# Prompt attention's transposed keys: one straight copy each, the swapped halves by on-chip transfers, and other places for a table load and four masks

## The chip, the cores and the metric

The kernel runs on one core of one Trainium2 chip. The metric is the device time of one execution in microseconds (us). A core has TensorE (PE, with its weight loads listed as PEld), VectorE (DVE), ScalarE (ACT), GpSimd (POOL) and SyncE (SP), which run their own instruction queues in order and meet through semaphores, and 16 DMA engines that all queues share.

## The reference, cut to what matters

One inference step of a two-layer decoder, for a prompt of 512 tokens and 8 sample tokens. Layer 0 is native sparse attention with 16 query heads of 64 dimensions in 4 groups that share a key and value head. The change concerns the prompt's attention alone. Each query sees three branches, which are gated and added:

```python
s_c = jnp.einsum('bqkgd,bckd->bkgqc', qg, kc) * scale       # compressed keys, 31 of them
p_c = masked_softmax(s_c, mask_c)
...
s_s = jnp.einsum('bqkgd,bkqnpd->bkgqnp', qrg, k_sel) * scale   # selected blocks
p_s = masked_softmax(s_s.reshape(...), mask_s)
...
s_w = jnp.einsum('bqkgd,blkd->bkgql', qrg, kw) * scale      # window of 512
p_w = masked_softmax(s_w, mask_w)
```

With 512 prompt tokens there are 8 blocks and 16 may be selected, so the selected branch and the window branch are both plain causal attention, over different keys (`kind` 0 and 1 below).

## The kernel before, in words

Layer 0's attention is a row of blocks: projections, compression of the cached keys, prompt attention, sample attention. At the end of each block all engines meet. The change is inside `stage_prompt_attention` (L2268).

**Units.** The softmax work is cut into 64 units, `NU`. A unit n is a pair of query heads (`hp`, 8 of them), a `kind` (0 or 1) and a query tile `i` of 128 rows, in the order 3, 0, 2, 1 (`unit`, L2321). So units 0 to 3 are kind 0 of the first pair, units 4 to 7 kind 1 of the first pair, and units 32 and up use key heads 2 and 3. The width of a unit is (i + 1) x 128 keys, hence 512, 128, 384 and 256. Both heads of a pair (`par` 0 and 1) are computed at once, one on the upper and one on the lower 64 rows of PE; so the transposed keys of a head, `kT`, 64 rows high, must exist in both halves of the 128 partitions.

**The path of a unit.** PE computes the scores (L2333) into one of three banks of PSUM; they wait for the DVE minimum of the unit before (L2330). DVE adds the causal mask and takes the minimum (L2487, the wait is on `scored`). ACT takes the exponential with its sum (L2546). DVE inverts the sum (L2494). POOL scales by the inverse and the gate (L2572). Four units later (`LAG`) PE turns the probabilities (L2347), DVE and ACT copy them back (L2430, L2522), and six or seven units later come the products with the values (L2364).

**Compressed branch.** Its scores for key head h are `scores_c(h)` (PE, L2394), its masks `mask_c(h)` (DVE, two additions per head, L2465), then `least_c`, `lower_c`, an exponential on ACT (L2551), `total_c`, `weight_c`, `weigh_c`. It is spread between the units.

**The opening.** PE turns the keys in four groups (L2387), one for each kind and pair of key heads, into four PSUM banks; rows 0 to 63 of a bank are the pair's first head, rows 64 to 127 its second. In the kernel before, DVE copies rows 0 to 63 of each bank to both halves of the first head's slot (L2457, eight copies of 64 rows), and ACT copies rows 64 to 127 to both halves of the second head's slot (L2529, eight copies), each bank after DVE has done with it. ACT then spreads the compressed values (L2532, four copies to `vcz`) and comes to its first exponential. PE's order is: compressed heads 0 and 1, unit 0, compressed head 2, unit 1, compressed head 3, units 2 and up. DVE does the masks of heads 0 and 1 after unit 1, that of head 2 after unit 2, that of head 3 after unit 3.

**SP's queue.** In this block SP first runs `cache.read_table(sp, "sp")` (L2577), which reads 4 x 8 = 32 page numbers from on-chip memory into registers (the value load is on L2697). Then it issues `first_selected` (16 transfers of 128 KB for the sample attention, L2712) and `first_windows` (L2715), and later ones behind semaphores of prompt attention's progress.

Of the kernel before, what the change touches and what calls it, by code (L numbers as in the profile page):

```python
# [19 lines left out]
P = 128  # L20
# [2247 lines left out]
def stage_prompt_attention(c, cache):  # L2268
# [10 lines left out]
    PR = 5  # L2279
    ORDER = (3, 0, 2, 1)  # L2280
    k_turned, k_kept, spread = c.sem("att_k_turned"), [c.sem("att_k_kept_dve"), c.sem("att_k_kept_act")], c.sem("attc_spread")
    cleared, v_spread = c.sem("attc_cleared"), c.sem("attc_v_spread")
    c_scored, c_masked, c_least, c_subbed, c_exped, c_link, c_weight, c_scaled, c_turned, c_kept = (
        c.sem(f"attc_{x}") for x in ("scored", "masked", "least", "subbed", "exped", "link", "weight", "scaled", "turned", "kept"))
# [4 lines left out]
    with ExitStack() as mine:  # L2289
# [16 lines left out]
        def wide(x):  # L2306
            return x.unsqueeze(2).to_broadcast([P, QT * GRP, KP])

        def score_bank(n, par):
            return (2 * n + par) % 3  # L2310

# [12 lines left out]
        with nc.Block() as block:  # L2324
            @block.tensor
            def _(pe):
                def scores(n):
                    hp, kind, i = unit(n)
                    if n >= 1:
                        pe.wait_ge(lowered, 2 * n - 1)  # L2330
                    for par in range(2):
                        rows = slice(par * HD, par * HD + HD)
                        mm = nc.tensor.matmul(ps[:, score_bank(n, par), 0:(i + 1) * P], c.qrT[rows, hp, i * P:(i + 1) * P],  # L2333
                                              kT[rows, kind, hp // 2, 0:(i + 1) * P], start=True, stop=True)
                    mm.then_inc(scored, 1)

                def turn(n):
# [51 lines left out]
                def scores_c(h):  # L2389
# [5 lines left out]
                                                  kcz[:, h].rearrange("p w k -> p (w k)"), start=True, stop=True)  # L2395
                    mm.then_inc(c_scored, 1)

                pe.wait_ge(spread, 2)
                scores_c(0)
                scores_c(1)  # L2400
                for e in range(2):
                    pe.wait_ge(k_kept[e], 4)
                scores(0)
                scores_c(2)
                for e in range(2):
                    pe.wait_ge(k_kept[e], 8)
                scores(1)
                scores_c(3)
                for n in range(2, NU + LAG_PV + 1):
                    if n < NU:  # L2410
                        scores(n)
                    if n == LAG:
                        pe.wait_ge(c_masked, 2 * NKV)
                    if LAG <= n < NU + LAG:
                        turn(n - LAG)
                    if n % (4 * QT) == 2 * QT and n < NU:
                        turn_c(n // (4 * QT))
                    for part in range(2):
                        m = n - LAG_PV - part
                        if m >= 0 and m % QT == QT - 1:  # L2420
                            values(m, part)

            @block.vector
            def _(dve):
# [25 lines left out]
                    dve.wait_ge(c_weight, h + 1)  # L2450
                    nc.vector.tensor_mul(rows_k(h), rows_k(h), wide(ctot[:, h])).then_inc(c_scaled, 1)

                for n in range(4):
                    kind, a = divmod(n, 2)
                    dve.wait_ge(k_turned, n + 1)
                    for to in range(2):
                        nc.vector.tensor_copy(kT[to * HD:(to + 1) * HD, kind, 2 * a, :], ps[0:HD, n, :]).then_inc(k_kept[0], 1)  # L2457
                def mask_c(h):

                    dve.wait_ge(c_scored, NKV)  # L2460
                    for j in range(2):
                        src = ps[:, 4 + h, j * QT * 2 * KP:(j + 1) * QT * 2 * KP].rearrange("p (t w k) -> p t w k", t=QT, w=2)
                        dst = sc[:, h].rearrange("p (t g k) -> p t g k", t=QT, k=KP)[:, :, 2 * j:2 * j + 2]
                        mask = c.cmask[:].rearrange("p (t k) -> p t k", t=QT).unsqueeze(2).to_broadcast([P, QT, 2, KP])
                        nc.vector.tensor_add(dst, src, mask).then_inc(c_masked, 1)  # L2465
# [13 lines left out]
                for n in range(NU + LAG):  # L2479
                    if n < NU:  # L2480
                        hp, kind, i = unit(n)
                        w = (i + 1) * P
                        dve.wait_ge(scored, n + 1)
                        for par in range(2):
                            if n >= PR:
                                dve.wait_ge(turned[par], n - PR + 1)
                            nc.vector.tensor_tensor_reduce(pr[:, n % PR, par, 0:w], ps[:, score_bank(n, par), 0:w], c.causal[:, SEQ - w:SEQ], 1.0,  # L2487
                                                           3e38, ALU.add, ALU.min, low[:, n % PR, par:par + 1]).then_inc(lowered, 1)
                    if n >= LAG:
                        keep_first(n - LAG)  # L2490
                    if 1 <= n <= NU:
                        m = n - 1
                        dve.wait_ge(exped, 2 * m + 2)
                        nc.vector.reciprocal(tot[:, m % PR], tot[:, m % PR]).then_inc(recip, 1)  # L2494
                    if n == 1:
                        mask_c(0)
                        mask_c(1)
                    if n == 2:
                        mask_c(2)
                    if n == 3:  # L2500
                        mask_c(3)
                    if n < NU:
                        h, r = divmod(n, 4 * QT)
                        if r == 1:
                            least_c(h)
                        if r == 2:
                            lower_c(h)
                        if r == QT:
                            total_c(h)
                        if r == QT + 1:  # L2510
                            weight_c(h)
                        if r == QT + 2:
                            weigh_c(h)

            @block.scalar
            def _(act):
                def keep_second(n):
                    act.wait_ge(turned[1], n + 1)
                    dst, src = turned_back(n, 1)
                    if n // QT >= 2:  # L2520
                        act.wait_ge(o_filled, n // QT - 1)
                    nc.scalar.copy(dst, src).then_inc(kept[1], 1)  # L2522

                for n in range(4):
                    kind, a = divmod(n, 2)

                    act.wait_ge(k_kept[0], 2 * (n + 1))
                    for to in range(2):
                        nc.scalar.copy(kT[to * HD:(to + 1) * HD, kind, 2 * a + 1, :], ps[HD:P, n, :]).then_inc(k_kept[1], 1)  # L2529
                act.wait_ge(cleared, 2)  # L2530
                for g in range(GRP):
                    nc.scalar.copy(vcz[32 * g:32 * g + NCP, :, g // 2, g % 2 * HD:(g % 2 + 1) * HD],  # L2532
                                   c.vcp[0:NCP, :].rearrange("p (h d) -> p h d", h=NKV)).then_inc(v_spread, 1)
                for n in range(NU + LAG_PV + 1):
                    if LAG <= n < NU + LAG:
                        keep_second(n - LAG)
                    if n % (4 * QT) == 2 * QT and n < NU:
                        h = n // (4 * QT)
                        act.wait_ge(c_turned, h + 1)
                        nc.scalar.copy(pcT[:, h, :], ps[:, 7, :]).then_inc(c_kept, 1)  # L2540
                    if n < NU:
                        hp, kind, i = unit(n)
                        w = (i + 1) * P
                        for par in range(2):
                            act.wait_ge(lowered, 2 * n + par + 1)
                            nc.scalar.activation(pr[:, n % PR, par, 0:w], pr[:, n % PR, par, 0:w], ACT.Exp, scale=-1.0,  # L2546
                                                 bias=low[:, n % PR, par:par + 1], accum_out=tot[:, n % PR, par:par + 1]).then_inc(exped, 1)
                    if n % (4 * QT) == QT - 1 and n < NU:
                        h = n // (4 * QT)
                        act.wait_ge(c_subbed, h + 1)  # L2550
                        nc.scalar.activation(sc[:, h], sc[:, h], ACT.Exp, scale=-1.0).then_inc(c_exped, 1)  # L2551
                    if n >= LAG_PV and (n - LAG_PV) % (2 * QT) == 0 and n > LAG_PV:
                        hp = (n - LAG_PV) // (2 * QT) - 1
                        act.wait_ge(o_filled, 2 * (hp + 1))
                        nc.scalar.copy(c.oT[:, hp, 0:SEQ], ps[:, 7, :]).then_inc(o_kept, 1)
# [20 lines left out]
            def _(sp):  # L2576
                cache.read_table(sp, "sp")  # L2577
                sp.wait_ge(c.h_stored, 16)
                cache.first_selected(sp)
                sp.wait_ge(k_turned, 4)  # L2580
                cache.first_windows(sp)
# [1421 lines left out]
```

## Time and profile before

| | us |
|---|---|
| median of 3 runs | 1520.79 |
| lowest and highest | 1518.48, 1522.76 |
| the profiled execution, its own time | 1520.4 |
| its span, first to last instruction | 1518.7 |
| PE busy, DVE busy, ACT busy | 1468.6, 872.3, 422.7 |

The profile is of one execution. The span is what the trace's clock covers; the execution's own time has some 1.7 us around it. Prompt attention lies between about 265 and 414 us of the span. Busy shares are means over stages with different limits; what counts for the change is which wait ends last in the stretch that it touches.

### The profile page before, as it was taken

What the parts mean: (1) busy time and instruction counts of PE and PEld (TensorE: products, weight loads), DVE (VectorE), ACT (ScalarE), POOL (GpSimd) and SP (SyncE); (2) the same over time, 40 slices, a digit from 0 to 9 for tenths busy, and PEclk for the clock granted to TensorE, in tenths of its full rate; (3) what the DMA queues carried; (4) which work ended last, traced back from release to release, by engine and by line L of the source; (5) the groups of instructions that cost most, each with busy time, mean ns of one, the idle gap of its engine ahead of it and who ended that gap; (6) DMA issues with size and microseconds to landing.
All of it is one profiled execution on the core that took longest, in us unless ns stands there. A gap on an engine that the chain in (4) does not pass through costs nothing. (4 is left out here: it accounts for less than half of the span.)

```text
span 1518.7 us, 25820 instructions
## 1 busy us (share of the span) xinstructions
PE 1468.6 (97%) x9697; PEld 1220.3 (80%) x9697; DVE 872.3 (57%) x1926; ACT 422.7 (28%) x1076; POOL 353.9 (23%) x478
## 2 busy tenths in 40 slices
PE   8999999899898999999999999899999999999998
PEld 7878899555565888888888888688888888888888
DVE  2754343778653796565567734671485556676513
ACT  3011343788630343333300000433441111000012
POOL 0000300466561339993000018280000000000000
PEclk9999999899999999999999999999999999999999
DMA  8445471311196626464343320703121312322201
GB/s 272 117 123 144 140 234 47 106 32 53 51 334 213 203 83 225 143 217 152 109 127 125 111 90 0 305 30 119 61 106 57 112 65 102 111 84 83 84 28 57
DMA packets 142893, 184.34 MB, mean 121 GB/s; under 512 B 31298, under 2 KB 101642, under 8 KB 141746
## 3 DMA queue, kind: packets, MB, share of 16 engines
q1 hardware_dynamic: 139634, 174.31, 35.2%
q0 software_dynamic: 3136, 8.39, 1.6%
q8 instruction: 77, 1.26, 0.3%
q14 instruction: 46, 0.38, 0.1%
HBM read 163.42 MB, written 29.69 MB: 127 GB/s over the span
## 5 line engine op out<-in xcount | busy, mean ns | idle before, releaser
L2572 POOL TENSOR_SCALAR att_p<-att_p,att_tot,gates 128x512 f32<-128x512 f32 (+3 forms) x128 | 79.4, 631 | 62.1 <-DVE att_tot L2494 62.1
L296 PE MATMUL psum<-xT,l_w 128*128 128x260 f32 x384 | 85.3, 383 | 2.0 <-PEq L113 1.8
L953 PE MATMUL psum<-xT,l_w 128*128 128x260 f32 x384 | 85.2, 383 | 1.6 <-PEq L113 1.6
L296 PEld LDWEIGHTS psum<-xT,l_w 128*128 128x128 f32 x384 | 72.8, 190 | 13.5 <-issue 2.4
L953 PEld LDWEIGHTS psum<-xT,l_w 128*128 128x128 f32 x384 | 72.8, 190 | 12.9 <-issue 1.8
L969 PE MATMUL psum<-l_up_t,l_w_sums 128*128 128x260 f32 x336 | 78.2, 382 | 0.0
L2487 DVE CUSTOM_DVE_ANT_0 att_p<-psum,causal 128x512 f32<-128x512 f32 (+3 forms) x128 | 57.4, 486 | 27.9 <-PE psum L2333 27.8
L2145 PE MATMUL psum<-cmp_xt,cmp_w 64*128 64x256 f32 (+1 forms) x640 | 72.2, 362 | 0.3 <-DVE cmp_xt L2066 0.3
L2546 ACT ACTIVATE att_p<-att_p,att_low 128x512 f32<-128x512 f32 (+3 forms) x128 | 70.8, 556 | 4.7 <-DVE att_low L2487 4.1
L969 PEld LDWEIGHTS psum<-l_up_t,l_w_sums 128*128 128x128 f32 x336 | 63.8, 190 | 9.8
L2333 PE MATMUL psum<-att_kT,qrT 64*128 64x512 f32 (+3 forms) x256 | 54.3, 503 | 14.1 <-DVE att_low L2487 13.9
L1232 ACT ACTIVATE l_hidden<-l_tmp 128x260 f32<-128x260 f32 x64 | 26.6, 420 | 144.9 <-DVE l_tmp L1382 144.8
L312 PE MATMUL psum<-xT,l_w 128*128 128x260 f32 x272 | 62.9, 382 | 0.0
L969 PE MATMUL psum<-xT,l_w 128*128 128x260 f32 x272 | 62.9, 382 | 0.0
L312 PE MATMUL psum<-l_up_t,l_up_w_sums 128*128 128x260 f32 x264 | 61.5, 382 | 0.0
L2145 PEld LDWEIGHTS psum<-cmp_xt,cmp_w 64*128 64x128 f32 x640 | 60.8, 187 | 0.6 <-DVE cmp_xt L2066 0.5
L969 PE MATMUL psum<-xT,l_w_sums 128*128 128x260 f32 x256 | 60.4, 382 | 0.0
L969 PEld LDWEIGHTS psum<-xT,l_w 128*128 128x128 f32 x272 | 51.7, 190 | 7.9
L1086 PE MATMUL psum<-l_hidden,l_w 128*128 128x260 f32 (+2 forms) x384 | 58.1, 311 | 0.0
L1715 PE MATMUL psum<-xT,proj_w 128*128 128x260 f32 x256 | 56.9, 383 | 0.7 <-DVE xT L1854 0.5
L312 PEld LDWEIGHTS psum<-xT,l_w 128*128 128x128 f32 x272 | 51.1, 190 | 7.5
L1086 PEld LDWEIGHTS psum<-l_hidden,l_w 128*128 128x128 f32 x384 | 53.8, 191 | 3.9
(584 smaller groups left out, 3179.9 us busy)
## 6 DMA issues: line engine op xcount, KB each, us to landing
l_w<-in_mlp_w SPq DMA_DIRECT2D x16, 2048.0 KB, 8.1
l_w<-in_mlp_w SPq DMA_DIRECT2D x32, 1024.0 KB, 5.1
proj_w<-in_nsa_w_in SPq DMA_DIRECT2D x4, 2048.0 KB, 10.4
cmp_raw<-in_cache_kv_cmp SPq DMA_DIRECT2D x24, 256.0 KB, 3.0
xT<-in_cache_kv_cmp SPq DMA_DIRECT2D x24, 256.0 KB, 3.0
sa_more<-in_cache_kv_sel POOLq DMA_DIRECT2D x44, 128.0 KB, 6.5
sa_more<-in_cache_kv_sel SPq DMA_DIRECT2D x34, 128.0 KB, 7.5
hT<-in_cache_kv_cmp SPq DMA_DIRECT2D x16, 256.0 KB, 3.0
```

Of the source, the lines that this page charges most:

```text
L296: mm = nc.tensor.matmul(ps[:, n % 8, 0:HALF], w[s][:, k, m * P:(m + 1) * P], src[:, kk, cols(h)], start=(kk == 0), stop=(kk == last))
L312: mm = nc.tensor.matmul(ps[:, bank, 0:HALF], left(k), right(k), start=(fresh and k == 0), stop=(ends and k == KC - 1))
L953: mm = nc.tensor.matmul(ps[:, n % 8, 0:HALF], w[s][:, k, m * P:(m + 1) * P], src[:, kk, cols(h)], start=(kk == 0), stop=(kk == last))
L969: mm = nc.tensor.matmul(ps[:, bank, 0:HALF], left(k), right(k), start=(fresh and k == 0), stop=(ends and k == KC - 1))
L1086: mm = nc.tensor.matmul(ps[:, LAST_BANKS[part][m], 0:width(part)], wt[:, k, at:at + P], hid[:, kk, PARTS[part]], start=(kk == 0), stop=(kk ...
L1232: nc.scalar.activation(hid[:, tile, cols(h)], tmp[:, i % 4], ACT.Square).then_inc(hid_done, 1)
L1715: mm = nc.tensor.matmul(ps[:, bank_of(step), 0:HALF], w[:, j, k, m * P:(m + 1) * P], c.xT[:, k, h * HALF:(h + 1) * HALF], start=(k == 0), ...
L2145: mm = nc.tensor.matmul(out, w1[z * HD:(z + 1) * HD, i % 2, t].rearrange("p r e -> p (r e)"), moving, start=(t == 0), stop=(t == STRIDE - 1))
L2333: mm = nc.tensor.matmul(ps[:, score_bank(n, par), 0:(i + 1) * P], c.qrT[rows, hp, i * P:(i + 1) * P], kT[rows, kind, hp // 2, 0:(i + 1) * ...
L2487: nc.vector.tensor_tensor_reduce(pr[:, n % PR, par, 0:w], ps[:, score_bank(n, par), 0:w], c.causal[:, SEQ - w:SEQ], 1.0, 3e38, ALU.add, AL ...
L2546: nc.scalar.activation(pr[:, n % PR, par, 0:w], pr[:, n % PR, par, 0:w], ACT.Exp, scale=-1.0, bias=low[:, n % PR, par:par + 1], accum_out= ...
L2572: ve.tensor_scalar(pr[:, n % PR, par, 0:w], pr[:, n % PR, par, 0:w], tot[:, n % PR, par:par + 1], c.gates[:, i, gate:gate + 1], ALU.mult, ...
```

## The change

1. Key copies. `kT` slot 2a now takes a straight copy of the bank of pair a (first head in the upper half, second head below), slot 2a + 1 the swapped one. `key_slot(h, par)` picks the slot. The bank of kind 0, pair 0 is copied in four half-height copies, two on DVE and two on ACT, in an order in which the two engines read different halves. The other three banks are copied once, full height, two by DVE and one by ACT; their swapped slots are filled by six SBUF-to-SBUF transfers of 64 partitions x 2 KB from SP's queue, placed after `read_table` and the wait for `h_stored`, ahead of `first_selected`.
2. Waits. PE waits for `near_swapped` (two transfers) ahead of unit 4 and for `far_swapped` (four) ahead of unit 32.
3. PE's order: unit 0 first, then compressed heads 0 and 1, unit 1, compressed heads 2 and 3, units 2 and up.
4. DVE's masks: head n after the minimum of unit n (n from 0 to 3), each waiting only for its own head's scores.
5. ACT: a one-column exponential at the head of the block, so that its table load comes there; the four spreading copies of the values go behind the exponentials of units 0 to 3.

```diff
+        def key_slot(h, par):
+            return h // 2 * 2 + (h % 2 ^ par)
...
-                                              kT[rows, kind, hp // 2, 0:(i + 1) * P], start=True, stop=True)
+                                              kT[rows, kind, key_slot(hp // 2, par), 0:(i + 1) * P], start=True, stop=True)
...
+                pe.wait_ge(k_kept[0], 3)
+                pe.wait_ge(k_kept[1], 2)
+                scores(0)
                 pe.wait_ge(spread, 2)
                 scores_c(0)
                 scores_c(1)
-                for e in range(2):
-                    pe.wait_ge(k_kept[e], 4)
-                scores(0)
+                pe.wait_ge(k_kept[0], 4)
+                scores(1)
                 scores_c(2)
-                for e in range(2):
-                    pe.wait_ge(k_kept[e], 8)
-                scores(1)
                 scores_c(3)
+                pe.wait_ge(k_kept[1], 3)
                 for n in range(2, NU + LAG_PV + 1):
+                    if n == 4:
+                        pe.wait_ge(near_swapped, 32)
+                    if n == 4 * 2 * QT:
+                        pe.wait_ge(far_swapped, 64)
...
-                for n in range(4):
+                dve.wait_ge(k_turned, 1)
+                for half in range(2):
+                    rows = slice(half * HD, (half + 1) * HD)
+                    if half == 1:
+                        dve.wait_ge(k_kept[1], 1)
+                    nc.vector.tensor_copy(kT[rows, 0, 0, :], ps[rows, 0, :]).then_inc(k_kept[0], 1)
+                for n in range(1, 3):
                     kind, a = divmod(n, 2)
                     dve.wait_ge(k_turned, n + 1)
-                    for to in range(2):
-                        nc.vector.tensor_copy(kT[to * HD:(to + 1) * HD, kind, 2 * a, :], ps[0:HD, n, :]).then_inc(k_kept[0], 1)
+                    nc.vector.tensor_copy(kT[:, kind, 2 * a, :], ps[:, n, :]).then_inc(k_kept[0], 1)
                 def mask_c(h):
 
-                    dve.wait_ge(c_scored, NKV)
+                    dve.wait_ge(c_scored, h + 1)
...
+                    if n < NKV:
+                        mask_c(n)
                     if 1 <= n <= NU:
...
-                    if n == 1:
-                        mask_c(0)
-                        mask_c(1)
-                    if n == 2:
-                        mask_c(2)
-                    if n == 3:
-                        mask_c(3)
...
-                for n in range(4):
-                    kind, a = divmod(n, 2)
-
-                    act.wait_ge(k_kept[0], 2 * (n + 1))
-                    for to in range(2):
-                        nc.scalar.copy(kT[to * HD:(to + 1) * HD, kind, 2 * a + 1, :], ps[HD:P, n, :]).then_inc(k_kept[1], 1)
-                act.wait_ge(cleared, 2)
-                for g in range(GRP):
-                    nc.scalar.copy(vcz[32 * g:32 * g + NCP, :, g // 2, g % 2 * HD:(g % 2 + 1) * HD],
-                                   c.vcp[0:NCP, :].rearrange("p (h d) -> p h d", h=NKV)).then_inc(v_spread, 1)
+                nc.scalar.activation(tot[:, 0, 0:1], c.eps[:], ACT.Exp).then_inc(exp_ready, 1)
+                act.wait_ge(exp_ready, 1)
+                act.wait_ge(k_turned, 1)
+                for to in range(2):
+                    if to == 1:
+                        act.wait_ge(k_kept[0], 1)
+                    nc.scalar.copy(kT[to * HD:(to + 1) * HD, 0, 1, :], ps[(1 - to) * HD:(2 - to) * HD, 0, :]).then_inc(k_kept[1], 1)
+                act.wait_ge(k_turned, 4)
+                nc.scalar.copy(kT[:, 1, 2, :], ps[:, 3, :]).then_inc(k_kept[1], 1)
...
+                    if n < GRP:
+                        if n == 0:
+                            act.wait_ge(cleared, 2)
+                        nc.scalar.copy(vcz[32 * n:32 * n + NCP, :, n // 2, n % 2 * HD:(n % 2 + 1) * HD],
+                                       c.vcp[0:NCP, :].rearrange("p (h d) -> p h d", h=NKV)).then_inc(v_spread, 1)
...
                 cache.read_table(sp, "sp")
                 sp.wait_ge(c.h_stored, 16)
+                for n, kept_by, count in ((2, 0, 4), (1, 0, 3), (3, 1, 3)):
+                    kind, a = divmod(n, 2)
+                    sp.wait_ge(k_kept[kept_by], count)
+                    for to in range(2):
+                        sp.dma_start(kT[to * HD:(to + 1) * HD, kind, 2 * a + 1, :],
+                                     kT[(1 - to) * HD:(2 - to) * HD, kind, 2 * a, :]).then_inc(near_swapped if n == 2 else far_swapped, 16)
                 cache.first_selected(sp)
```

## Rows read from the trace of the kernel before

**Rows 1.** The page, busy time, share of the span and instructions of each engine.

```profile
PE 1468.6 (97%) x9697; PEld 1220.3 (80%) x9697; DVE 872.3 (57%) x1926; ACT 422.7 (28%) x1076; POOL 353.9 (23%) x478
```

**Rows 2.** Timeline, 265 to 285 us: start, duration, engine, line, operation [idle before].

```profile
265.89 5.69 DVE L2457 COPY att_kT<-psum 64x512 f32<-64x512 f32 x8 [1.17 <-PE psum L2387]
...
267.14 3.79 PE L2394 MATMUL psum<-attc_kcz,qT 128*128 128x64 f32 x32
267.33 1.19 ACT L2529 COPY att_kT<-psum 64x512 f32<-64x512 f32 x2 [4.65 <-DVE att_kT L2457]
...
270.86 1.13 PE L2333 MATMUL psum<-att_kT,qrT 64*128 64x512 f32 x4
...
272.82 1.69 ACT L2532 COPY attc_vcz<-vcp 31x256 f32<-31x256 f32 x4
...
274.53 1.28 ACT L2546 ACT_TABLE_LOAD   x1
...
277.37 0.17 DVE L2494 RECIPROCAL att_tot<-att_tot 128x2 f32<-128x2 f32 x1 [2.48 <-ACT att_p L2546]
277.46 1.39 DVE L2465 TENSOR_TENSOR qT<-psum,cmask 128x256 f32<-128x256 f32 x4
...
280.18 0.70 PE L2333 MATMUL psum<-att_kT,qrT 64*128 64x256 f32 x4 [3.07 <-DVE att_low L2487]
...
281.84 0.41 DVE L2487 CUSTOM_DVE_ANT_0 att_p<-psum,causal 128x256 f32<-128x256 f32 x1
...
282.32 2.08 PE L2333 MATMUL psum<-att_kT,qrT 64*128 64x512 f32 x4 [1.44 <-DVE att_low L2487]
...
284.45 0.69 DVE L2487 CUSTOM_DVE_ANT_0 att_p<-psum,causal 128x512 f32<-128x512 f32 x1 [1.11 <-PE psum L2333]
```

**Rows 3.** SP's queue, 265 to 296 us: page-number loads (durations in ns), first transfers.

```profile
L2697 SPq TENSOR_LOAD <-pages x32: 261/267/275, 265.2 to 282.1; - x32
...
282.85 13.03 SPq L2712 DMA_DIRECT2D hT<-in_cache_kv_sel  x16
```

**Rows 4.** Transfers: issue (ns min/median/max), landing (us), by tile; last, the page's row.

```profile
L1645 SPq DMA_DIRECT2D proj_tmp<-qT x16: 507/591/755, 33.6 to 67.4; - x16
...
DMA to landing us min/median/max: 1.9/2.0/2.5
...
L1645 SPq DMA_DIRECT2D q_swapped<-qT x16: 507/590/754, 36.2 to 74.8; - x16
...
DMA to landing us min/median/max: 2.0/4.6/8.0
...
hT<-in_cache_kv_sel SPq DMA_DIRECT2D x16, 128.0 KB, 2.2
```

**Rows 5.** Windows: stretch, length, busy times, granted clock, DMA share, GB/s.

```profile
265.00:284.00 19.00, 14.26 (x100) 10.99 (x102) 13.22 (x38) 12.75 (x30) 5.89 (x10) 0.92 0.01 2
...
295.00:405.00 110.00, 101.55 (x1006) 57.35 (x1004) 83.70 (x349) 89.25 (x287) 67.71 (x110) 1.00 0.18 54
...
282.00:291.00 9.00, 7.34 (x52) 0.50 0.43 122
291.00:292.00 1.00, 0.69 (x12) 0.83 0.83 264
```

**Rows 6.** Timeline, 292 to 326 us: minima of units 8, 20 and 24, scores at full clock.

```profile
292.97 0.69 DVE L2487 CUSTOM_DVE_ANT_0 att_p<-psum,causal 128x512 f32<-128x512 f32 x1 [0.48 <-PE psum L2333]
...
299.58 1.13 PE L2333 MATMUL psum<-att_kT,qrT 64*128 64x512 f32 x4 [0.29 <-DVE att_low L2487]
...
316.85 0.69 DVE L2487 CUSTOM_DVE_ANT_0 att_p<-psum,causal 128x512 f32<-128x512 f32 x1 [0.48 <-PE psum L2333]
...
325.41 0.69 DVE L2487 CUSTOM_DVE_ANT_0 att_p<-psum,causal 128x512 f32<-128x512 f32 x1 [0.48 <-PE psum L2333]
```

**Rows 7.** Timeline, 285 us: full-height copies of 512 from PSUM, ACT and DVE.

```profile
285.29 0.59 ACT L2522 COPY att_pT<-psum 128x512 f32<-128x512 f32 x1 [1.38 <-PE psum L2347]
...
285.68 0.69 DVE L2430 COPY att_pT<-psum 128x512 f32<-128x512 f32 x1
```

More of the change, by code:

```diff
@@ L2281, in stage_prompt_attention @@
     k_turned, k_kept, spread = c.sem("att_k_turned"), [c.sem("att_k_kept_dve"), c.sem("att_k_kept_act")], c.sem("attc_spread")
+    exp_ready = c.sem("att_exp_ready")
+    near_swapped, far_swapped = c.sem("att_k_near_swapped"), c.sem("att_k_far_swapped")
     cleared, v_spread = c.sem("attc_cleared"), c.sem("attc_v_spread")
```

## Prediction

> **What bounds the kernel now.** I read the page's busy times first [rows 1]: TensorE (PE) is busy 97% of the span. The edit touches one block, prompt attention, so the rest was read there alone. The windows say that in its long middle part, 295 to 405 us, PE is busy 101.55 of 110 us [rows 5]. Heads and query tiles follow each other in 64 units n; each unit runs scores (PE), minimum (VectorE, DVE), exp (ScalarE, ACT), reciprocal (DVE), scaling (GpSimd, POOL), and PE turns it four units later. A unit's scores wait for the DVE minimum of the unit before. So this middle part has one rhythm, and whatever comes late at unit 4 pushes all the later units.
>
> The opening is another matter. The timeline of 265 to 285 us [rows 2] reads so: DVE copies keys in eight half-height copies until 271.58, ACT follows it behind a chain, PE starts the first scores at 270.86, ACT spends 1.69 us on the spread of the values and 1.28 us on a table load, and the first exp comes only at 275.82. DVE waits 2.48 us for it, does its masks, and PE stands still for 3.07 us and again 1.44 us. Unit 4's scores start at 282.32, at the end of that chain. This is the stretch that the edit reorders.
>
> The third view is the one that decides: SyncE (SP), which must issue the new transfers. From 265.2 us it reads 32 page numbers into registers, the last at 282.1, and its first transfer goes out at 282.85 [rows 3]. That is (282.85 - 265.2) / 32 = 0.55 us per page number. The new code puts the transfers behind `read_table` in the same in-order queue.
>
> **The change part by part.**
>
> *Copies of the keys.* Removed: 16 half copies, on DVE 8 x 0.71 = 5.69 us, on ACT 8 x 0.59 = 4.76 us [rows 2]. Added: on DVE two halves of 0.68 and two full-height ones; on ACT two halves of 0.58 and one full. The full-height price is that of the turned-back copies, 0.69 us on DVE and 0.59 us on ACT for 128x512 [rows 7]. DVE: 2.8 us instead of 5.7, ACT: 1.8 instead of 4.8.
>
> *Table load at the head of ACT's queue.* The load of 1.28 us moves to where ACT now idles (its row says it idled until DVE's copy at 267.33). The one-column exp is not in the trace; below nothing there is no case, above it costs at most the 128-wide shape's share of a unit; I take 0.2 us. ACT is then free at 265.1 + 1.3 + 0.2 = 266.6. Its first half ends at 267.2, DVE's second half at 267.9, then DVE's full copies at 268.6 and 269.3, ACT's second half at 267.8 and its full one at 268.4. DVE and ACT now read two halves of one PSUM bank at once; no row shows that pair. If they ran one after the other instead, 0.7 us would be added. I take none, since what follows hides either.
>
> *Order on PE.* The scores of unit 0 need three DVE copies and two of ACT: 268.7, against 270.86. PE idles 1.6 us before them (it did compressed scores there, 3.79 us for two heads [rows 2]). Then compressed heads 0 and 1 until 273.7, unit 1 until 274.1, heads 2 and 3 until 278.0, unit 2 until 278.9. Before, unit 2's scores had run at 276.2; the gain of the early start is spent here.
>
> *Masks and the spread of values.* Four masks of 0.35 x 2 us each only change places [rows 2] (the row of 1.39 us is two heads); the spread's four copies go between exps. DVE: unit 0 from 269.9, mask 0, unit 1 at 274.2, mask 1, reciprocal at 275.6 (exp 0 is done by 272.2, not 277.2), unit 2 at 279.0, mask 2, `lower_c`, unit 3 at 281.5. Before, unit 3 came at 281.84. Here the whole rearrangement is worth about 0.3 us, bounds 0 and 1 us: DVE and PE had the same work in the same 17 us, only in another order.
>
> *The transfers.* Two "near" ones, 64 partitions x 2 KB = 128 KB each, must have landed before unit 4's scores; four "far" ones before unit 32's, some 55 us later, so they cost nothing. Their issues, with the near ones 6 x 0.59 = 3.5 us, push SP's first selected pages from 282.85 to about 286.4; their cover is the rest of the block, since SP next waits for semaphores of units far behind, and the pages are read only after the block. Price of one issue: 0.507 to 0.755 us, median 0.59 [rows 4]. Time to landing: on-chip copies of 65 KB took 1.9 to 2.5 (median 2.0) in one buffer and 2.0 to 8.0 (median 4.6) in the other, loads of 128 KB from HBM at the very place in the queue where these will go took 2.2 [rows 4]. I take 2.2, as from 265 to 284 us the DMA engines are idle (share 0.01 [rows 5]) and the size is the same.
>
> *The new wait.* The near transfers have their data by 269.4, but go out at 282.8 and 283.4. The second lands at 283.4 + 2.2 = 285.6; with 0.1 us for PE to pick it up, unit 4's scores start at 285.7 instead of 282.32: **+3.4 us**. Behind this wait on PE's queue stand scores 4, turn 0, scores 5 and all the rest; behind those, DVE's minimum 4, the reciprocal of unit 3 (it stands after minimum 4 in DVE's queue), POOL's scaling of unit 3. None of them can run ahead of it, so the stall is not made up.
>
> *Can the middle part make it up?* PE has 8.45 us idle in 110, in small gaps that belong to the unit's own loop. Units 4 to 8 took 292.97 - 284.45 = 8.52 us and units 20 to 24, with the same companions, 325.41 - 316.85 = 8.56 [rows 2, 6]. The rhythm does not get faster when there is backlog. After the block all engines meet, and later stages only shift.
>
> *TensorE's clock.* The mean of 0.92 over 265 to 284 says that it fell to 1.2 GHz at about 281 (2 x 0.08 x 19 = 3.0 us before 284), after PE's waits of 3.07 and 1.44 us around a burst of 0.70 us; it stayed at 0.50 from 282 to 291 and came back to 2.4 GHz within 291 to 292 [rows 5]. Scores of 512 took 2.08 us at the low clock [rows 2] and 1.13 at the full one [rows 6]: 0.95 us in the chain, while the four units after lost nothing (8.52 against 8.56). In the new kernel PE idles from about 280.2 to 285.7, so I expect the fall again ahead of unit 4 and the same 0.95 us paid as before: nothing to add.
>
> The Trainium skill, "TensorE: Matmul & The Clock Gate", section "Part 1: The HAM clock gate (the "warmup" mystery)", has it that the throttled clock is the default and that activity releases it. By that rule the longer wait makes the low clock at the resumption surer: the sum stays +3.4, where a clock that held (rival C) would give +2.45. The trace agrees so far, since its fall followed idle time of PE.
>
> Sum: 0 (opening, swallowed by the wait) + 3.4 = +3.4 us. The profiled execution took 1520.4 us around a span of 1518.7; the median of the runs is 1520.79, which is 0.4 more. On the median: 1524.2 us, ratio 1.0022. About 0.3% (4.6 us) is what this kernel's measurement can tell from no change, so this counts as no change.
>
> **The rivals.**
>
> *A, the transfers land late (slower by over 0.3%).* If the near transfers behave like the second buffer's copies, 4.6 us instead of 2.2, unit 4 starts at 283.4 + 4.6 + 0.1 = 288.1: +5.8 us, 1526.6; at 8.0 us +9.2. It decides from a landing time of 283.4 + x + 0.1 - 282.32 = 4.6, so x = 3.4 us. For it: same kind of copy, twice the bytes, and four far transfers issued right behind. Against it: those copies had weight loads in flight, these have idle engines. 17 in 100, and 6 more in 100 for the forecast's own sum coming out above the bound by several small excesses in issue and pickup.
>
> *B, the wait is hidden.* If SP is earlier than I read it, or the order in PE's queue covers it, only the opening's rearrangement is left: -0.3 us, bounds -1 and 0, 1520.5. Speaks against it: the row of 32 register loads. 7 in 100.
>
> *C, the clock holds.* If PE is still at 2.4 GHz when the transfers land (it now works without the 3.07 us gap until 278.9), unit 4's scores take 1.13 instead of 2.08 us: 3.4 - 0.95 = +2.45, 1523.2. If it falls later, inside the full rhythm, some of it is lost again. 13 in 100.
>
> *D, the opening's gain goes through (faster by over 0.3%).* The first exp comes 5.0 us earlier (272.2 - 277.2 at its end). If POOL's and ACT's early results shortened the loop of all later units, 5 us could come off: 1515.8. Nothing in the order of the queues lets unit 4 start before minimum 3. 3 in 100.
>
> **How the numbers follow.** Forecast 54 in 100 inside the bound and 6 above; A 17, B 7, C 13, D 3. Faster 0.03; same 0.54 + 0.07 + 0.13 = 0.74; slower 0.17 + 0.06 = 0.23. The range from 1520.5 (B) to 1527.5 (A's median and some more) leaves out D, B's lower half and A's long landings, under 2 in 10.
>
> **What would show it.** SP's first transfer is `att_kT<-att_kT` at about 282.8, two of them landing by 285.6; PE's L2333 group has one wait of about 5.4 us that ends with a DMA, where before a 1.44 us one ended with DVE; the first exp at about 270.6; the table load at about 265.1, under other waits; minimum of unit 4 at about 287.8 (284.45 before), that of unit 8 at about 296.3; the selected pages leave after 286; all stages after the block as long as before. Wrong would be: unit 4 waiting for DVE instead of a transfer (B), a landing above 3.4 us (A), minimum 4 at 286.9 (C), a block that is shorter from unit 4 to its end (D), or a time lost or won after the block, of which I count nothing.

## The result and the profile after

The changed kernel takes 1527.87 us in the median of 8 runs (1524.41 to 1532.0), the kernel before 1521.45 beside it; the ratio is 1.0038, interval 1.0027 to 1.0049. That is 0.0038 x 1521 = 5.8 us slower, just beyond the 0.3% that the prediction set as its bound; 3.4 us were forecast. A second measurement on one chip, beside other variants, gave 1.0046 (1.0029 to 1.0063), below.

The timeline of the changed kernel, the lines that answer to [rows 2] (start, duration, engine, line, operation [idle before]):

```profile
265.55 1.28 ACT L2533 ACT_TABLE_LOAD   x1 [2.52 <-PEq L2074]
...
265.58 1.94 PE L2392 MATMUL psum<-ident,kv 128*128 128x128 f32 x16 [0.31 <-PEq L2074]
...
266.84 0.20 ACT L2533 ACTIVATE att_tot<-eps 128x1 f32<-128x1 f32 x1
...
269.16 1.13 PE L2338 MATMUL psum<-att_kT,qrT 64*128 64x512 f32 x4 [1.64 <-DVE att_kT L2471]
...
270.22 3.79 PE L2399 MATMUL psum<-attc_kcz,qT 128*128 128x64 f32 x32
...
271.07 0.72 ACT L2554 ACTIVATE att_p<-att_p,att_low 128x512 f32<-128x512 f32 x1 [2.21 <-DVE att_low L2501]
...
281.33 0.41 DVE L2501 CUSTOM_DVE_ANT_0 att_p<-psum,causal 128x256 f32<-128x256 f32 x1
...
283.10 3.92 SPq L2596 DMA_DIRECT2D att_kT<-att_kT  x6
...
286.06 2.08 PE L2338 MATMUL psum<-att_kT,qrT 64*128 64x512 f32 x4 [5.70 <-DMA att_kT<-att_kT]
...
288.18 0.69 DVE L2501 CUSTOM_DVE_ANT_0 att_p<-psum,causal 128x512 f32<-128x512 f32 x1 [5.35 <-PE psum L2338]
...
295.53 2.02 PE L2338 MATMUL psum<-att_kT,qrT 64*128 64x512 f32 x4 [0.30 <-DVE att_low L2501]
```

The opening went as forecast: table load first, first exp at 271.07 instead of 275.82, unit 3's minimum at 281.33. Then PE stands still for 5.70 us, and a transfer ends it. The block began 0.35 us later in this execution, so I measure from the first key turn of each trace, 265.58 here. Before it was this row:

```profile
265.23 1.94 PE L2387 MATMUL psum<-ident,kv 128*128 128x128 f32 x16 [0.31 <-PEq L2074]
```

Unit 4's scores start after 17.09 us before [rows 2] and after 20.48 us here, **+3.39 us**; the forecast was 3.4. The transfers' own rows (issue in ns, landing in us, minimum/median/maximum):

```profile
L2596 SPq DMA_DIRECT2D att_kT<-att_kT x6: 462/586/597, 283.1 to 286.4; - x6
...
DMA to landing us min/median/max: 2.3/2.4/2.5
```

In this execution the block lost more than that. SP's last window load of the block waits for the scores of all 64 units. First the row of before, then that of the changed kernel, then that of a second profile of the changed kernel (`e9_after` below, first key turn at 265.01):

```profile
404.98 0.39 SPq L2715 DMA_DIRECT2D sa_early<-in_cache_kv_win  x1
```

```profile
409.72 0.39 SPq L2734 DMA_DIRECT2D sa_early<-in_cache_kv_win  x1
```

```profile
408.27 0.39 SPq L2734 DMA_DIRECT2D sa_early<-in_cache_kv_win  x1
```

It leaves 139.75 us after the first key turn before, and 144.14 us here: +4.39. In the second profile it is 143.26: +3.51, hardly more than the wait. So the further 1.0 us belongs to one execution of two. It goes with TensorE's clock. Unit 8's scores, the last row of the timeline, took 2.02 us here and 1.13 us before. The windows of the changed kernel (length, busy times, granted clock, DMA share, GB/s):

```profile
282.00:284.00 2.00, 0.00 (x0) 0.00 (x0) 0.83 (x5) 1.91 (x6) 1.22 (x3) 0.93 0.00 0
284.00:296.00 12.00, 8.30 (x58) 5.49 (x60) 6.86 (x28) 5.44 (x18) 4.08 (x7) 0.50 0.68 176
296.00:298.00 2.00, 2.00 (x21) 0.81 (x19) 0.62 (x3) 0.63 (x4) 1.30 (x2) 0.66 0.60 193
298.00:404.00 106.00, 97.33 (x970) 55.55 (x970) 82.12 (x339) 86.18 (x275) 64.26 (x104) 1.00 0.18 58
...
464.00:475.00 11.00, 11.00 (x103) 3.62 (x105) 1.96 (x4) 0.00 (x0) 0.63 (x2) 0.53 1.05 361
```

The clock (0.50 is 1.2 GHz) fell at about 283.7 and came back at about 297.4, so it held the resumed work for 11.3 us after 286.06 and took unit 8's wide scores in; before it was back by 292 [rows 5], in time for them. In the second profile it was low from 282.1 to 288.9 and from 292.4 to 295.8, and units 4 to 8 took no longer than before (minimum to minimum 8.54 us; 9.43 in the first profile, 8.52 before). The last window is a second fall, in the sample attention at 464 to 474.5 us, which the profile of before did not have: SP's weight load of the next stage stands 22.87 us after the previous one's place there (459.31 to 482.18) and 26.86 here (463.79 to 490.65), 4.0 us more. So the profile's +9.2 us of span is 0.35 ahead of the block, 4.39 in it, 4.0 in the sample attention's clock and 0.5 in the rest. The medians differ by 6.4 us, so about a third of this is not the change.

### The profile page after: what moved, and what is told of

It reads as the page before. It is cut to its first block and busy times, and to the rows that moved or that the text cites. A ratio compares the mean times of both kernels' runs of the same rounds, so it can differ in the third digit from the quotient of the medians.

```text
span 1527.9 us, 25823 instructions
## 1 busy us (share of the span) xinstructions
PE 1473.8 (96%) x9697; PEld 1221.2 (80%) x9697; DVE 870.7 (57%) x1922; ACT 420.3 (28%) x1072; POOL 353.8 (23%) x478
```

## The experiments

All times are ratios to the kernel before on the same chip, five rounds each. "Unit 4" is the start of its scores after the first key turn. Single executions list their mean granted clock, which is used below. Runs `e0` to `e3` share one chip, `e4` to `e7` a second, `e8` to `e10` a third; only runs of one chip were measured side by side.

The profiles side by side, one execution each. The block is the time from the first key turn to the last window load. The last column is when TensorE's clock was low in the block (us of that trace; the block begins at 264.7 to 265.6, in `e1` and `e2` at 267.6 and 268.0).

| run | unit 4, us | block, us | clock low |
|---|---|---|---|
| before | 17.09 | 139.75 | 281.1 to 291.3 |
| `e0_before` | 17.10 | 139.80 | 278.6 to 285.4, 288.8 to 292.2 |
| changed | 20.48 | 144.14 | 283.7 to 297.4 |
| `e9_after` | 20.47 | 143.26 | 282.1 to 288.9, 292.4 to 295.8 |
| `e2_before_wait` | 20.47 | 144.11 | 282.6 to 299.7 |
| `e1_near_first` | 23.66 | 146.43 | 272.6 to 299.9 |
| `e4_order` | 14.79 | 138.57 | 278.9 to 282.3, 285.8 to 292.6 |
| `e5_gap_awake` | 16.31 | 139.37 | 287.4 to 294.2 |
| `e3_awake` | 32.19 | 153.27 | 269.9 to 290.3 |
| `e6_awake_twice` | 20.45 | 143.31 | 290.3 to 297.1 |
| `e10_table` | 15.96 | 139.52 | 278.4 to 292.1 |
| `e7_near_act` | 14.70 | 137.84 | 280.6 to 290.9 |
| `e8_act_awake` | 14.70 | 135.78 | never |

The clock fell somewhere in the block in every profile but the last. What the variants change is when, for how long, and over which work.

**Unchanged kernels again.** Is the second fall the change's?

> The kernel before once more, unchanged, for the granted clock of each execution. If the fall of TensorE's clock at 464 us in the changed kernel's profile is a matter of chance, single executions here spread between clock 0.986 and 0.994 too, with times 4 us apart; if the change brings it, all are at 0.992 or above. The ratio is 1.000 within 0.001.

Before against before: 1.0008 (0.9995 to 1.0021), 12 executions from 1519.9 us (clock 0.995) to 1527.7 (0.988), unit 4 at 17.10. Its own profile has the fall in the sample attention that the first profile had not:

```profile
452.00:458.00 6.00, 4.49 (x37) 3.39 (x37) 3.87 (x8) 1.25 (x2) 5.78 (x11) 1.00 1.07 347
458.00:469.00 11.00, 10.51 (x93) 3.68 (x97) 2.45 (x5) 0.00 (x0) 1.61 (x3) 0.57 1.05 358
```

The one program falls there or not. Of the 13 profiles of this study 7 have it, with and without the change. It costs some 4 us when it comes (26.86 against 22.87 above), and the kernel before has it too. Whether the change makes it more frequent is not shown.

> The changed kernel once more, unchanged, beside the others on one chip and with the clock of each execution. Theory: the opening's pause lets the clock fall in some executions here too, so that the lowest times are 3.4 us above before's lowest and the highest 5 us above its highest; ratio 1.003 to 1.0045. Rival (only the wait counts): the spread is that of before, ratio 1.002 to 1.0025.

1.0046 (1.0029 to 1.0063), unit 4 at 20.47. Six executions: 1527.9 to 1532.5 at clocks 0.992 to 0.986; those of before beside them 1519.3 to 1528.3 at 0.995 to 0.988. The ratio lies just beyond what the theory gave (1.0045 at most). The low end moved by 8.6 us, not 3.4, and the high end by 4.2; six executions beside 23 say little about the ends. In its profile the opening ran at the full clock, so the fall that the theory names is not in it. Unit 4's scores and unit 8's minimum:

```profile
285.48 2.08 PE L2338 MATMUL psum<-att_kT,qrT 64*128 64x512 f32 x4 [5.69 <-DMA att_kT<-att_kT]
...
296.14 0.69 DVE L2501 CUSTOM_DVE_ANT_0 att_p<-psum,causal 128x512 f32<-128x512 f32 x1 [1.23 <-PE psum L2338]
```

**The wait alone.**

> The kernel before, its copies and orders untouched, plus six transfers of the same size at the place of the changed kernel's, and TensorE's two waits for them. They rewrite keys with equal values, so nothing of the computation changes. Theory (the wait alone makes the loss): unit 4's scores start at 285.7 to 286.1, the time is 3.4 to 6.5 us above before, ratio 1.002 to 1.0043. Rival (the new order of the opening adds to the loss): ratio below 1.0015 here.

```diff
+                    if n == 4:
+                        pe.wait_ge(near_swapped, 32)
...
+                for kind, slot in ((1, 0), (1, 1), (0, 2), (0, 3), (1, 2), (1, 3)):
+                    sp.dma_start(kT[HD:P, kind, slot, :], kT[0:HD, kind, slot, :]).then_inc(near_swapped if slot < 2 else far_swapped, 16)
                 cache.first_selected(sp)
```

```profile
288.42 2.08 PE L2334 MATMUL psum<-att_kT,qrT 64*128 64x512 f32 x4 [4.29 <-DMA att_kT<-att_kT]
```

Ratio 1.0032 (1.0015 to 1.0050). Unit 4 comes 20.47 us after the first key turn (267.95): the same place as in the changed kernel, although nothing of the opening was moved. The far transfers and the wait for them ahead of unit 32 are added as well. So the place of the transfers in SP's queue alone sets unit 4's start, and what the new opening gains ahead of it ends in this wait. Its block, 144.11 us, is that of the first profile of the changed kernel (144.14), long fall of the clock included: unit 8's scores took 2.01 us here too. Between this ratio and the changed kernel's 1.0038 and 1.0046 the intervals do not separate anything.

**The near transfers ahead of the page numbers.**

> The changed kernel with the two near transfers ahead of the 32 page-number loads in SyncE's queue. Theory (the 5.7 us wait of unit 4 is SyncE's queue position): they go out at about 269.5 us and land by 273, unit 4's scores start at 281.7 to 282.1 instead of 286.06, and the time is 3.7 us or more below the changed kernel's, 1519.5 to 1522.5, ratio to before 0.999 to 1.001. Rival (the wait is cheap, the loss comes from elsewhere, such as the DMA engines or the order of the opening): unit 4's scores still later than 283.5 or the time still at ratio 1.003 or more.

```diff
+                swap(2, 0, 4)
                 cache.read_table(sp, "sp")
                 sp.wait_ge(c.h_stored, 16)
+                swap(1, 0, 3)
+                swap(3, 1, 3)
```

Ratio 1.0012 (0.9994 to 1.0030). The time came out beside the theory's 1.001, the place of unit 4 did not: the wait for a transfer is gone, yet unit 4 comes at 23.66, which meets the rival's condition (later than 283.5 in the changed kernel's trace), and the rival's "order of the opening" is where it comes from. The 12 executions fall in two groups, seven from 1519.1 to 1524.3 us at clocks 0.991 to 0.996, five from 1526.9 to 1530.9 at 0.986 to 0.988. The profile is of the second:

```profile
271.14 1.13 PE L2338 MATMUL psum<-att_kT,qrT 64*128 64x512 f32 x4 [1.64 <-DVE att_kT L2471]
272.20 6.78 PE L2399 MATMUL psum<-attc_kcz,qT 128*128 128x64 f32 x32
278.91 0.80 PE L2338 MATMUL psum<-att_kT,qrT 64*128 64x128 f32 x4
279.64 7.09 PE L2399 MATMUL psum<-attc_kcz,qT 128*128 128x64 f32 x32
```

```profile
273.00:299.00 26.00, 22.98 (x119) 18.41 (x120) 12.01 (x49) 10.21 (x32) 6.66 (x10) 0.50 0.25 60
```

After the opening's pause of 1.64 us the clock fell, and four heads of compressed scores took 13.9 us instead of 7.6. This pause is new in the changed kernel's order; I had counted it at nothing. Only this one execution of the upper group was profiled, and 2.3 us of its time were lost ahead of the block (first key turn at 267.56), where the clock was low too (0.60 from 184 to 188 us). That the other four fell in the opening is read from their clocks and times.

**Is it the pause?** Two kernels, both on top of the last one.

> Near transfers ahead of the page-number loads, and compressed head 0's scores ahead of unit 0 on TensorE, so that it no longer stands still for 1.64 us there. Theory (in e1_near_first that pause let the clock fall in five executions of twelve, and 15 us of compressed scores ran at 1.2 GHz): no execution with the clock at 0.988 or less by more than before has them, all within 1518.5 to 1525, ratio to before 0.997 to 0.9995. Rival (the falls come from TensorE's later waits, whatever the opening's order): single executions at 1529 to 1531 remain, ratio 1.001 or more.

```diff
+                pe.wait_ge(spread, 2)
+                scores_c(0)
                 pe.wait_ge(k_kept[0], 3)
                 pe.wait_ge(k_kept[1], 2)
                 scores(0)
-                pe.wait_ge(spread, 2)
-                scores_c(0)
                 scores_c(1)
```

Ratio 0.9998 (0.9989 to 1.0007), 11 executions from 1519.3 to 1523.2 us; unit 4 at 14.79.

> e1_near_first with six matmuls of 128x128 into a free PSUM bank in the 1.64 us pause of the opening, the order untouched. Theory (the pause, not the order, brings the fall): as e4_order, no executions at 1529 or more, median 1 to 3 us below e1_near_first's. Rival: the same two groups of times, about 1521 and 1530, as in e1_near_first.

```diff
+                keep_awake(c, 4, 6)
                 pe.wait_ge(k_kept[0], 3)
```

`keep_awake(c, bank, n)` issues n matmuls of no use into an unused bank; below they are called fills. Ratio 0.9995 (0.9981 to 1.0009), 11 executions from 1520.3 to 1526.2 us, none below clock 0.993; unit 4 at 16.31. Both remedies take the upper group away: no execution of 22 is above 1526.3 us, where five of twelve were above 1526.8. So the pause most likely makes it; these two ran on another chip than `e1_near_first`. The theory's ratio for `e4_order` was missed by a little: 2.3 us earlier at unit 4 bought at most 1.7 us. Its profile has the reason: the clock fell twice behind the opening, and the block is only 1.18 us shorter than before.

**The clock in the changed kernel.**

> The changed kernel with 36 matmuls of 128x128 into an unused PSUM bank ahead of unit 4's wait, so that TensorE works for about 5.2 us instead of standing still. Theory (some 2 to 3 us of the loss is TensorE's clock falling in and after the wait): granted clock 1.00 from 280 to 300 us, unit 4's scores 1.13 us instead of 2.08, unit 8's minimum at most 10.6 us after unit 4's scores start (11.55 in the changed kernel), time 1.5 to 2.5 us below the changed kernel's. Rival (the clock costs nothing here, or the second fall at 464 us is independent of it): within 1 us of the changed kernel.

```diff
                     if n == 4:
+                        keep_awake(c, 3, 36)
                         pe.wait_ge(near_swapped, 32)
```

Ratio 1.0064 (1.0039 to 1.0089): a failed dose. The 36 matmuls ran 9.72 us, longer than the wait, and in its profile the clock had fallen at 270 us, in the opening, so unit 4 came at 32.19. What it shows: the opening's fall happens with the transfers at their late place too. The opening there is the changed kernel's, word for word. And with the clock up behind its fills, units 4 to 8 took 7.79 us from minimum to minimum (298.16 to 305.95).

> The changed kernel, its transfers behind the page-number loads, with six matmuls in the opening's pause and 20 ahead of unit 4's wait (36 were twice too many in e3_awake: each takes 0.25 us at the full clock). Theory (3.4 us of the loss is the wait, the rest the clock): unit 4's scores still start 20.4 to 21 us after the first key turn, but take 1.13 us; ratio to before 1.000 to 1.0018. Rival (the clock is no part of the loss): ratio 1.003 or more, as the changed kernel.

```diff
+                keep_awake(c, 4, 6)
                 pe.wait_ge(k_kept[0], 3)
...
                     if n == 4:
+                        keep_awake(c, 3, 20)
                         pe.wait_ge(near_swapped, 32)
```

```profile
279.52 4.73 PE L119 MATMUL psum<-ident 128*128 128x128 f32 x40
285.26 1.13 PE L2338 MATMUL psum<-att_kT,qrT 64*128 64x512 f32 x4 [1.01 <-DMA att_kT<-att_kT]
```

The 20 fills of the second place stand as 40 records. Unit 4 at 20.45, the wait untouched, its scores at the full clock. But the fall was put off, not taken away:

```profile
290.00:297.00 7.00, 6.68 (x54) 4.26 (x50) 5.38 (x20) 3.99 (x13) 4.06 (x6) 0.52 0.59 163
```

```profile
293.06 2.08 PE L2338 MATMUL psum<-att_kT,qrT 64*128 64x512 f32 x4 [0.30 <-DVE att_low L2503]
```

Unit 8's scores ran at the low clock, and the block lost 3.56 us against before. Ratio 1.0021 (1.0012 to 1.0030): 3.2 us. The ratio is a little above the 1.0018 of the theory and below the rival's 1.003, which the interval reaches. Beside the changed kernel's 1.0038 and 1.0046 it is 1.7 to 2.5 parts in a thousand less, 2.6 to 3.8 us. The mean clocks of its executions are higher (0.992 to 0.998, against 0.986 to 0.992), so this went with the clock; but the intervals overlap slightly at their ends, the measurements are of different chips, and in which stretches it was won is not shown.

**One part alone, and a better kernel.**

> The kernel before with one part of the change alone: the one-column exponential at the head of ScalarE's queue. Theory (ScalarE is on the chain there, and its row of the table load is 1.28 us): first exp 1.28 us earlier, unit 4's scores about 15.8 us after the first key turn (17.09 before), ratio 0.9988 to 0.9995. Rival (the compressed masks on VectorE bound the chain): unit 4's scores at 16.8 us or later and ratio 0.9996 or more.

Ratio 0.9985 (0.9972 to 0.9999), unit 4 at 15.96, first exp 9.31 us after the first key turn instead of 10.59: 1.28 us earlier, the table load's own length. The theory's 15.8 holds for unit 4; the ratio's interval takes in its 0.9988 to 0.9995. In the profile itself only 0.23 us of it is left at the block's end: the clock was low until 292.1, and unit 8's scores took 2.00 us.

> The changed kernel with the two near transfers replaced by two half copies on ScalarE (2 x 0.58 us, done by about 271 us), no wait for a transfer ahead of unit 4, and compressed head 0's scores ahead of unit 0. Theory: as e4_order within 1 us, unit 4's scores 16.3 to 17.1 us after the first key turn, ratio 0.997 to 0.9995. Rival (the copies on ScalarE delay the first exp and with it the chain): unit 4's scores at 17.1 us or later and ratio 1.000 or more.

```diff
+                act.wait_ge(k_kept[0], 4)
+                for to in range(2):
+                    nc.scalar.copy(kT[to * HD:(to + 1) * HD, 1, 1, :], ps[(1 - to) * HD:(2 - to) * HD, 2, :]).then_inc(k_kept[1], 1)
```

Ratio 0.9989 (0.9977 to 1.0001). Unit 4 at 14.70, as in `e4_order` (14.79) and better than the range given; the two copies fit ahead of the first exp (they end at 270.76, it starts at 271.17). That the missing pause makes it better is argued.

> e7_near_act with short fills for TensorE's pauses: 2 matmuls ahead of unit 3's scores, 5 ahead of unit 4's, 5 ahead of unit 6's. Theory (what e7_near_act still loses in the block is the clock between 280 and 291 us): granted clock 1.00 there, block 1 us shorter, ratio to before 0.9975 to 0.999, below e7_near_act's 0.9989. Rival (the fills are paid for, or the clock falls elsewhere): ratio 0.999 or more.

```diff
+                    if n in (3, 4):
+                        keep_awake(c, 3, (2, 5)[n - 3])
+                    if n == 6:
+                        keep_awake(c, 7, 5)
```

```profile
265.00:290.00 25.00, 22.67 (x202) 17.60 (x202) 18.74 (x66) 17.87 (x49) 11.03 (x18) 1.00 0.19 47
290.00:404.00 114.00, 104.80 (x1042) 59.25 (x1042) 86.70 (x361) 92.26 (x295) 69.76 (x113) 1.00 0.22 68
```

```profile
281.14 0.69 DVE L2503 CUSTOM_DVE_ANT_0 att_p<-psum,causal 128x512 f32<-128x512 f32 x1
...
288.93 0.69 DVE L2503 CUSTOM_DVE_ANT_0 att_p<-psum,causal 128x512 f32<-128x512 f32 x1 [0.48 <-PE psum L2338]
```

Ratio 0.9973 (0.9959 to 0.9987): 4 us faster than before and 11 us faster than the changed kernel beside it. The clock holds through the block; SP's last window load leaves at 401.04 after a first key turn at 265.26, 135.78 us, 3.97 less than before and 2.06 less than in `e7_near_act`, where the theory gave 1. Units 4 to 8 took 7.79 us from minimum to minimum, as in `e3_awake`. The interval overlaps that of `e7_near_act` (another chip), so the gain of the fills rests on the profiles; that this version beats before and the changed kernel is clear.

## Why the prediction was right and where it was wrong

*The bound and the deciding row.* Right. Unit 4 waits for a transfer that stands behind 32 page numbers; `e2_before_wait` gives the same place with the copies and the order of before.

*The size of the wait.* Right: 20.48 against 17.09 us, 3.39 for 3.4. The terms were near (issue 0.586 for 0.59, landing 2.4 for 2.2, first issue at 283.10 with a block 0.35 later). The second profile of the changed kernel has the rest of the block as forecast too: minimum 8 stands at 296.36 on the scale of before (296.14 there, its block 0.22 us earlier), 296.3 was given.

*The whole kernel's time.* 5.8 us for 3.4, beyond the bound. The prediction gave 6 in 100 to its own sum coming out above, by excesses in issue and pickup; those were not the cause. Of the 2.4 us between, the first profile has 1.0 in the block and the second 0.1. The rest is not shown: profiles exist for one execution of each measurement, and their other differences from before (the fall in the sample attention) come and go without the change. So the place inside the range, 1526.6 us on the prediction's base, is partly luck.

*The opening swallowed.* Right for the wait: unit 3's minimum came 0.9 us earlier on the block's own scale (15.75 against 16.61), inside the bounds, and unit 4 did not notice.

*"... while the four units after lost nothing (8.52 against 8.56)."* This step failed. Units 20 to 24 were no measure for units 4 to 8: between them run TensorE's products with the values (L2364, the first at 294.7 us) and one with the compressed values (L2372, 1.13 us), which units 4 to 8 do not have. Units 4 to 8 themselves take 7.79 us where the clock held (`e3_awake`, `e8_act_awake`). So the low clock already cost the kernel before 0.73 us there, beside the 0.95 in unit 4's scores. The sum was not touched, since a cost paid on both sides drops out; the price of the clock was.

*"... so I expect the fall again ahead of unit 4 and the same 0.95 us paid as before: nothing to add."* Half right. The fall came ahead of unit 4 in both profiles. In the second it cost what it had cost before; in the first it lasted until 11.3 us after unit 4's start instead of some 9, unit 8's wide scores fell into it, and the block lost 1.0 us more. `e2_before_wait` has a long fall with the old opening (unit 8's scores 2.01 us), `e10_table` one of 13.7 us with the old opening and no wait for a transfer (2.00 us). So a long fall needs neither the new order nor the wait; that the wait makes it more likely is not shown.

*"PE idles 1.6 us before them"* was put down as harmless. The clock can fall behind that pause with most of the compressed scores still to come: seen in the profiles of `e1_near_first` and `e3_awake`, and gone from the times in `e4_order` and `e5_gap_awake`. `e3_awake` has the changed kernel's opening, so it can happen there; neither of the changed kernel's own two profiles caught it. Its executions at clocks 0.986 to 0.989 are no evidence: five of the seven of `e2_before_wait`, which has no such pause, lie at 0.987 to 0.989 too. How much of the changed kernel's loss it makes stays open. The step that failed is the one that added nothing for this pause; the 3.4 us do not depend on it.

*Rivals.* A (late landing) named the side on which the time came out, and even its 1526.6, but by a mechanism that did not occur: 2.4 us, not 3.4 or more. B and D did not occur. C did not occur in either profile of the changed kernel; `e6_awake_twice` brought its condition about, unit 4's scores at 1.13 us, and its block still lost 3.56 us and not 2.45, since the clock fell later, as C's own last sentence allows. A rival "the clock falls in the opening" was missing, and its price could have been read from the rows: the compressed scores doubled.

The Trainium skill, "TensorE: Matmul & The Clock Gate", "Part 1: The HAM clock gate (the "warmup" mystery)", says that the throttle's phase is not tied to the kernel's start, so that the same kernel differs from run to run. The runs agree that it differs: one program, clock 0.988 to 0.995, 1519.9 to 1527.7 us. That the phase is the reason no run here shows.

The Trainium skill's "DMA: Bandwidth & Descriptors", "Issuing engines are not separate DMA queues", says that issuing from several engines only saves the sequencer's time, usually small beside the transfer. Here that time was not small: the transfers' data was ready at about 269.7 us, and SP's queue held them until 283.10, 13 us for a transfer of 2.4. `e1_near_first` took the wait away by order within the one queue; no run issued them from another engine.

## What to carry to other kernels

A transfer is as late as what stands ahead of it in its issuer's queue; register loads stand in no list of busy work, so read the issuing engine's own rows before a computing engine is made to wait for it. A pause that is moved on TensorE is priced by the work behind it at half the clock, weighted by how often the clock falls; what the low clock already costs is read from the same units at the full clock, not from others. Where single executions of one program spread by several us, list their granted clocks before a cause is read from two profiles.

## What the runs showed that I had not expected

- A pause of 1.64 us was followed by a fall in the profile of `e1_near_first`, and by their clocks in four more of its twelve executions. From 298 to 404 us of the changed kernel, with pauses of 0.3 to 0.5 us ahead of the scores, the clock stayed at 1.00.
- In twelve executions of one kernel the mean clock and the time go together: 0.995 with 1519.9 us, 0.988 with 1527.7.
- Useless matmuls of 1.4 us or less in TensorE's pauses made the block 2.06 us shorter (135.78 against 137.84 us). The ratios, 0.9973 with them and 0.9989 without, point the same way with overlapping intervals.
- With fills in some of TensorE's pauses the clock did not hold, it fell later: at 287.4 us in `e5_gap_awake` and 290.3 in `e6_awake_twice`. With fills ahead of units 3, 4 and 6 and no pause in the opening it held through the block (`e8_act_awake`).
